# Three norms split around their turn: raw x is turned, weights enter at the turned block, the root at the product

## The reference

```python
def rms_norm(x, g):
    y = x * lax.rsqrt(jnp.mean(x * x, axis=-1, keepdims=True) + EPS)
    return y * g

# first block
h = rms_norm(x, norm_attn)
proj = h @ w_in                    # q_mla | ckv | k_rope | qkv_dil | gate_pre
o_mla, o_dil = mla_branch(...), dilated_branch(...)
gates = sigmoid(gate_pre + b_gate)
x = x + (gates[0] * (o_mla @ w_o_mla) + gates[1] * (o_dil @ w_o_dil)) @ w_out
h2 = rms_norm(x, norm_ffn)
x = x + hier_moe(h2, ...)          # router on h2: 4 groups, 32 experts, 2 per token

# second block, layer 0 even, layer 1 odd
h = h + attn_retention_mixer(rmsnorm(h, norm_mix[0]), even_w_in, even_w_out)
h = h + peer(rmsnorm(h, norm_ffn[0]), ...)     # 8 heads x 16 gathered rows per token
h = h + short_conv_mixer(rmsnorm(h, norm_mix[1]), ...)
h = h + peer(rmsnorm(h, norm_ffn[1]), ...)
return rmsnorm(h, final_norm)
```

## Time and profile before

| | |
|---|---|
| median of 3 runs | 2150.3 us (2147.6 to 2150.67) |
| profiled execution, its own time | 2149.94 us |
| span of the profiled execution | 2148.1 us |
| mean granted clock of TensorE | 0.970 |
| PE busy | 1849.5 us (86%) |
| DVE, ACT, POOL busy | 1285.7, 714.7, 663.4 us |
| chain that ended last | DMA 32%, DVE 17%, issue 9%, PE 8% |

### The profile page before, as it was taken

One profiled execution on the slowest core, in us unless ns is written; L12 is line 12 of the kernel. 1 busy time (PEld: TensorE's weight loads), 2 busy tenths in 40 slices (PEclk: granted clock), 3 DMA queues, 4 the chain that ended last, 5 costly groups with the idle time before them and its releaser, 6 DMA issues.

```text
span 2148.1 us, 20313 instructions
## 1 busy us (share of the span) xinstructions
PE 1849.5 (86%) x5992; PEld 871.0 (41%) x5992; DVE 1285.7 (60%) x3071; ACT 714.7 (33%) x2002; POOL 663.4 (31%) x593
## 2 busy tenths in 40 slices
PE   9999999997899999999868887677888867888876
PEld 4445555332245445454423333323433433334322
DVE  1333433221122768666478797987777888777765
ACT  1232221111111346344334333433333343444442
POOL 2121001110000334334334353454334345444432
PEclk9999999999999999999999999899999999999998
DMA  7432366999796999999999999999999999999996
GB/s 247 168 119 77 144 247 254 409 418 419 324 357 242 378 421 393 421 416 421 421 422 421 420 411 421 407 401 421 421 421 421 420 411 415 421 421 420 415 421 283
DMA packets 114801, 779.40 MB, mean 363 GB/s; under 512 B 16048, under 2 KB 17760, under 8 KB 21632
## 3 DMA queue, kind: packets, MB, share of 16 engines
q0 software_dynamic: 78928, 542.37, 61.4%
q1 hardware_dynamic: 32256, 225.65, 26.3%
q10 hardware_dynamic: 3504, 10.04, 1.2%
HBM read 780.10 MB, written 10.49 MB: 368 GB/s over the span
## 4 chain that ended last, share of the span: by engine, by line
DMA 32%; DVE 17%; issue 9%; PE 8%; POOL 5%; ACT 2%; DVEq 0%; POOLq 0%; ACTq 0%
DMA arena<-in_c_rows_dram,arena 32%; DVE arena L2732 8%; POOL arena L2829 5%; PE banks L2718 3%; PE banks L1824 2%; DVE x L2738 2%; PE banks L369 1%; DVE arena L2637 1%; DVE arena L2628 1%; PE banks L1915 1%; DVE arena L2631 1%; ACT arena L2795 1%; DVE arena L2673 1%; DVE arena L2666 1%; DVE arena L2670 1%
## 5 line engine op out<-in xcount | busy, mean ns | idle before, releaser
L2718 PE MATMUL banks<-arena 128*128 128x512 f32 x1784 | 892.2, 630 | 225.9 <-ACT arena L2795 222.4
L2829 POOL DMA_INDIRECT arena<-in_c_rows_dram,arena x512 | 585.8, 1144 | 839.9 <-PE banks L2718 481.8
L2732 DVE CUSTOM_DVE_ANT_0 arena<-arena,xn 128x1024 f32<-128x1024 f32 x512 | 625.8, 1223 | 302.0 <-DMA arena<-in_c_rows_dram,arena 296.8
L2718 PEld LDWEIGHTS banks<-arena 128*128 128x128 f32 x1784 | 320.6, 195 | 684.0 <-ACT arena L2795 414.9
L2786 ACT ACTIVATE small<-small 128x1 f32<-128x1 f32 x512 | 103.5, 202 | 732.7 <-DVE small L2732 728.7
L314 PE MATMUL banks<-ring,hT 128*128 128x512 f32 (+1 forms) x480 | 202.1, 577 | 0.0
L2795 ACT ACTIVATE arena<-ident,small 128x128 f32<-128x128 f32 x446 | 179.1, 401 | 42.0 <-ACT small L2789 1.5
L376 ACT COPY arena<-banks 128x512 f32<-128x512 f32 (+4 forms) x218 | 101.0, 492 | 254.9 <-PE banks L360 107.4
L2789 ACT ACTIVATE small<-small 128x1 f32<-128x1 f32 x512 | 150.8, 295 | 49.0 <-DVE arena L2644 0.4
L314 PEld LDWEIGHTS banks<-ring,hT 128*128 128x128 f32 x480 | 87.9, 191 | 100.2 <-issue 98.4
L402 POOL TENSOR_TENSOR small<-small 128x1 f32<-128x1 f32 (+4 forms) x24 | 33.4, 1391 | 285.1 <-DVE small L398 266.0
(11 more groups left out here) (319 smaller groups left out, 1799.9 us busy)
## 6 DMA issues: line engine op xcount, KB each, us to landing
arena<-in_c_experts_dram SPq DMA_DIRECT2D x51, 1024.0 KB, 20.1
ring<-in_c_w_in_dram SPq DMA_DIRECT2D x30, 1024.0 KB
ring<-in_c_experts_dram SPq DMA_DIRECT2D x30, 1024.0 KB
ring<-in_c_w_q_dram SPq DMA_DIRECT2D x18, 1024.0 KB
ring<-in_c_odd_w_in_dram SPq DMA_DIRECT2D x15, 1024.0 KB
ring<-in_c_even_w_in_dram SPq DMA_DIRECT2D x12, 1024.0 KB
arena<-in_c_even_w_in_dram SPq DMA_DIRECT2D x10, 1024.0 KB, 17.3
arena<-in_c_rows_dram,arena POOLq DMA_INDIRECT x512
```

The lines of the kernel that those rows point to most:

```text
L2718: r = e.matmul(banks[:, bank_of[("acc", L, c, hf)], :], diag[:, diag_of[m], :], rows[:, row_of[m], D + hf * 512:D + (hf + 1) * 512], start ...
L2732: e.tensor_tensor_reduce(u, u, xn[:, c, :], 1.0, 0.0, ALU.mult, ALU.add, hid3[:, c, h, k:k + 1]).then_inc(ve.sem, ve.up(("u", p)))
L2829: e.indirect_dma_start(rows[:, b, :], None, table_uv, bass.IndirectOffsetOnAxis(ap=eix[:, c, 16 * h + k:16 * h + k + 1], axis=0)).then_inc ...
```

## The change

Norms "attn", "ffn" and "mix0" are split. x itself is turned (`pe_turn_half`), the gain, now a value per partition of the turned block (`gT_all`, 12 KB, loaded once), is multiplied in when the turned block is copied to `hT` (`act_gained`, four operations of one block each; `dve_gained`, one operation of four blocks), and the root is multiplied in when the product's bank is emptied (`act_rooted`, `scalar_tensor_tensor` on VectorE). The row copies of the gain for "attn" and "mix0" are no longer loaded. For the stored rows of the router, VectorE writes x * gain by halves (`times_gain`) and ScalarE multiplies by the root (`normed`).

At the start the identity is loaded before x. In the router the first chunk's turn stands inside the third half product, its router product before the fourth, its choice beside the fourth, and the rank product between that product's two parts; four idle products behind the first router are gone. Before the even mixer three idle products behind the addition are gone.

```diff
+        def act_gained(e, n, c, k):
+            name = ("hT", n, c, k)
+            g = fetched("gains")
+            e.wait_ge(g.sem, g.at("all"))
+            e.wait_ge(pe.sem, pe.at(name))
+            for i in range(4):
+                e.activation(hT[:, k + i, c * P:(c + 1) * P], banks[:, bank_of[name], i * P:(i + 1) * P], ACT.Copy,
+                             scale=gain_T[n][:, k + i:k + i + 1]).then_inc(ac.sem, ac.up(name))
+
+        def dve_gained(e, n, c, k):
+            e.tensor_tensor(hT[:, k:k + 4, c * P:(c + 1) * P], turned(name, P, 4),
+                            gain_T[n][:, k:k + 4].unsqueeze(2).to_broadcast([P, 4, P]),
+                            ALU.mult).then_inc(ve.sem, ve.up(name))
+
+        def act_rooted(e, name, dst, src, n, c):
+            await_root(e, n, c)
+            e.wait_ge(pe.sem, pe.at(name))
+            e.activation(dst, src, ACT.Copy, scale=ssn[n][:, c:c + 1]).then_inc(ac.sem, ac.up(name))
...
             ready(e, 1)
-            a2 = half(1, 0)
+            a2 = half(1, 0, first_turned)
             rings.drop(a2)
-            pe_turn_chunk(e, n, 0, xn[:, 0, :])
-            mid0(e)
-            a3 = half(1, 512)
-            mid1(e)
+            router(e, 0)
+            a3 = half(1, 512, ranked)
             rings.drop(a3)
-            pe_turn_chunk(e, n, 1, xn[:, 1, :])
+            turn_added(e, 1, 0)
+            turn_added(e, 1, 4)
+            router(e, 1)
...
             add(0, 0)
+            times_gain(0, 0)
             add(0, 512)
-            dve_norm(e, n, 0)
+            times_gain(0, 512)
+            mean(0)
+            dve_gained(e, n, 0, 4)
             add(1, 0)
-            dve_turned_chunk(e, n, 0)
+            times_gain(1, 0)
+            chosen(e)
+            ranked(e)
             add(1, 512)
-            e.wait_ge(ac.sem, ac.at(("sq", n, 1)))
-            dve_mean(e, ssn[n][:, 1:2], D, ("ms", n, 1))
-            mid0(e)
-            dve_normed(e, n, 1)
-            mid1(e)
-            dve_turned_chunk(e, n, 1)
+            dve_gained(e, n, 1, 4)
+            mean(1)
+            times_gain(1, 512)
...
+            square(0)
+            act_gained(e, n, 0, 0)
+            normed(0)
+            act_gained(e, n, 1, 0)
+            chain(e, ac)
+            square(1)
+            normed(1)
...
             elif s == GAIN_AT:
-                e.wait_ge(ve.sem, ve.at(("xn", "ffn", 1)))
+                e.wait_ge(ve.sem, ve.at(("xg", "ffn", 1)))
+                e.wait_ge(ac.sem, ac.at(("sq", "ffn", 1)))
...
             pe_idle_work(e, "results", 8, still)
-            e.wait_ge(ve.sem, ve.at(("x", "mix0", 0)))
-            pe_idle_work(e, "results added", 3, still)
             tensor_even(e)
```

More of the change, by code:

```diff
@@ L442, in sp_residual, with pe_residual, half @@
                     load(e, ("res" + n, c0, k), w[c0 // 256 + k // 4])
-        def pe_residual(e, n, lhs, second, mid0, mid1, ready):
-            def half(c, c0):
+        def pe_residual(e, n, lhs, second, ready, router, ranked):
+            def half(c, c0, between=None):
                 name = ("res" + n, c0, "c", c)
@@ L483, in add, with times_gain, mean @@
                 emptied[name] = (ve.sem, ve.n)
+            def times_gain(c, c0):
+                g = fetched("gain_" + n)
+                e.wait_ge(g.sem, g.at("all"))
+                chain(e, ve)
+                e.tensor_tensor(xn[:, c, c0:c0 + 512], x[:, c, c0:c0 + 512], gain[:, gain_of[n], c0:c0 + 512],
+                                ALU.mult).then_inc(ve.sem, ve.up(("xg", n, c)))
+            def mean(c):
+                e.wait_ge(ac.sem, ac.at(("sq", n, c)))
+                dve_mean(e, ssn[n][:, c:c + 1], D, ("ms", n, c))
@@ L1006, in scalar_first @@
         def scalar_first(e):
-            gain_fetch(e, "attn")
+            g = fetched("gains")
+            e.dma_start(gT_all, a["c_gains"]).then_inc(g.sem, g.up("all", by=16))
             for c in range(2):
@@ L1414, in router @@
                 r.then_inc(pe.sem, pe.up(("lg", c)))
-            def first_router(e):
-                router(e, 0)
-                pe_idle_work(e, "norm", 4, still)
-            still = rw.rearrange("p k n -> p (k n)")
-            pe_residual(e, "ffn", hT, second, nothing, first_router, ready)
-            router(e, 1)
-            rings.drop(("lg", 0))
-            rings.drop(("lg", 1))
             def bank(name):
@@ L1428, in bank, with ranked @@
                 return b
-            b = bank(("rank", 0))
-            e.wait_ge(fetched("tri").sem, fetched("tri").at("all"))
-            e.wait_ge(po.sem, po.at("ones"))
-            e.wait_ge(ve.sem, ve.at(("Ms", 0)))
-            e.matmul(banks[:, b, 0:32], tri, Ms[:, 0, :], start=True, stop=True).then_inc(pe.sem, pe.up(("rank", 0)))
+            def ranked(e):
+                b = bank(("rank", 0))
+                e.wait_ge(fetched("tri").sem, fetched("tri").at("all"))
+                e.wait_ge(po.sem, po.at("ones"))
+                e.wait_ge(ve.sem, ve.at(("Ms", 0)))
+                e.matmul(banks[:, b, 0:32], tri, Ms[:, 0, :], start=True, stop=True).then_inc(pe.sem, pe.up(("rank", 0)))
+            still = rw.rearrange("p k n -> p (k n)")
+            pe_residual(e, "ffn", hT, second, ready, router, ranked)
+            rings.drop(("lg", 0))
+            rings.drop(("lg", 1))
             b = bank(("rank", 1))
@@ L1561, in whose_place, with chosen @@
                                          ALU.is_equal, ALU.mult), ("hots", c))
-            first = choose(0)
-            def some(n):
-                for _ in range(n):
-                    next(first, None)
-            dve_residual(e, "ffn", lambda e: some(3), lambda e: some(5))
-            for _ in first:
-                pass
-            e.wait_ge(po.sem, po.at("ids"))
-            whose_tile(0)
+            def chosen(e):
+                for _ in choose(0):
+                    pass
+                e.wait_ge(po.sem, po.at("ids"))
+                whose_tile(0)
+            dve_residual(e, "ffn", chosen, lambda e: whose_place(0))
             for _ in choose(1):
                 pass
-            whose_place(0)
             whose_tile(1)
```

134 lines of the change are left out of this document (87 added, 47 removed).

## The result

The changed kernel took 2151.97 us (median of 20 runs, 2148.57 to 2155.75), the kernel before 2147.97 in the same sessions (20 runs, 2145.44 to 2152.26). The ratio is 1.0015, with an interval (95%) of 1.0009 to 1.0022: slower by 0.15%, some 3.2 us (the two medians lie 4.0 apart). I had forecast 2.9 us faster. Single executions of either kernel spread over 7 us, so I read the places in the profiles, not only the end.

A forecast was written before the change was run, and what follows sets the result against it. TensorE was taken to bound the first block, weight DMA the experts, both the mixer; 0.9 - 0.3 + 1.8 + 0.5 = 2.9 us gained gave 2147.4 us, range 2142.3 to 2151.8.

The forecast's parts named there:

- Even mixer: Before the even mixer: TensorE gets 2.9 us ahead, then waits for columns 1024's load; 0.5 us gain kept.
- the loads of this stage start only when the results have landed, which the change does not move: Even mixer: weight loads start no earlier, so of TensorE's 2.9 us lead only 0 to 1.6 is left.
- Router: Router: earlier second choice and gather let TensorE turn rows 2.1 us earlier; 1.8 us gained, ends 4.5 gained and 1.6 lost.
- I take 5.8: Router: the first gather, sharing engines with 2 MB of loads, lands in 5.8 us, between 3.4 unloaded and 9.6 loaded.
- I take off 0.3: Router: allowance of 0.3 us for TensorE's lower clock, which could lengthen the first expert products by up to 1.7.
- the router gives nothing: Rival at the router: late store and gather among 2 MB take all the gain; 2149 to 2150.8 us, chance 0.20.
- The mixer's gain is kept: Rival at the even mixer: columns 1024 land well before TensorE, 2.9 us gained instead of 0.5; 2145.0 us, chance 0.26.
- Start: Attention norm at the start: turning raw x brings the first product from 11.22 to 10.3 us; 0.9 us gained.
- Scaled unloads: Bank unloads with the root: each ScalarE one costs 0.09 us more, mostly beside TensorE; 0.3 us lost.
- The waits that I had priced: Attention pairs: TensorE waits for ScalarE's copies 8 times for 3.7 us; scaled unloads there lose nothing to 1.5 us.
- that rival: Rival on ScalarE: scaled copies reload its table, 1.28 us per switch; 2159 us, chance 0.04.
- The fourth rival: Rival in the last 1440 us, a chain of row gathers: another load order costs some us; 2155 us, chance 0.06.

The follow-up runs named there:

- e5: Changed kernel with four loads not needed before 685 (2.0 MB) issued behind ScalarE's exponentials and unloads, not ahead of its first unload; ratio 1.0011.
- e8: Changed kernel with the even mixer's weight stream released when the first chunk's expert results have landed, not both chunks'; ratio 0.9991.
- e9: Kernel before with the even mixer's weight stream released by the first chunk's expert results alone; ratio 0.9994.
- e1: Kernel before with only the attention norm split, router and even mixer as before; ratio 0.9999.
- e3: Kernel before with only the even mixer's norm split and the three idle products left out; ratio 1.0009.
- e6: Kernel before with four loads (next norm's gain, keys, second mixer's gain, convolution's weights) moved behind ScalarE's exponentials and unloads; ratio 0.9999.
- e11: Changed kernel with the two 1 MB expert weight loads held until the first gathered rows have landed; ratio 0.9990.
- e2: Kernel before with only the router's norm split and its order changed; ratio 0.9997.
- e12: Changed kernel with both the two 1 MB loads held behind the first gather and the stream released by the first chunk's results; 2142.5 us, ratio 0.9964.

## Why the prediction was wrong

Four terms made the sum. The steps that failed are the mixer's release of the stream, and in the router the landing of the gather and the price of the clock.

- **Even mixer: 0.5 gained, in fact 2.3 lost in the profile (C to D), 2.0 on the mean (113.7 in nine kernels with it and the old release of the stream, 111.7 in six without).** The first half of the mechanism stood: TensorE came 3.0 us ahead and waited for columns 1024. What failed is "the loads of this stage start only when the results have landed, which the change does not move". Counted from C, which is what a head start of TensorE is counted from, it moved: the stream started 1.2 later. I also stopped at the first wait. The next tile that TensorE stood for, the second one of columns 2560, began 62.5 after C. Before, 60.4 after C was early enough (both tiles of 2560 run from 650.66 for 7.03 us without a wait). Some 0.6 of the rest may be ScalarE's loads, which go out earlier (e5); what remains is not explained. That the stream's release is the limit is shown by e8 against e9: 2.2 gained with it moved.
- **Router: 1.8 gained, in fact 1.3 lost at B, 1.7 on the mean (A to B 62.9 in eight kernels with it alone, from 60.3 to 63.7, and 61.2 in before, e1, e3, e6 and e9, from 59.7 to 61.9).** The chain up to the gather went as written: second store at 352.27, gather released by the store, issued 3.2 earlier after A on the mean (2.5 forecast). Two steps behind it failed. The first is the landing, "I take 5.8": from its issue to the turn it was 7.2 in the profile and 8.0 on the mean of the eight (up to 9.0). So the turn, 2.1 earlier by the forecast, came 1.65 earlier in the profile (50.8 after A and not 52.5) and 0.4 on the mean. The second is "I take off 0.3" for the clock. The idle products' weight loads ran at the full clock, took 4.18 us instead of the 6.93 that I had used, and left TensorE idle for 4.6. In the kernel before they had run at 0.50. Behind the wait it was the work that ran at 0.50: 0.94 lost on the turn, 1.06 on the products behind it, 0.98 on the up-projection, together 3.0 us (2.2 on the mean). The rival "the router gives nothing" was right in its outcome and, on the mean, in its reason (the late landing takes most of the gain); it did not foresee the clock. "The mixer's gain is kept" was not right. e11 shows that the two loads are what the gather waits for: held back, it is there in 3.5 us. The rule of the Trainium skill that loads of all issuers interleave on the same engines (DMA: Bandwidth & Descriptors, Issuing engines are not separate DMA queues) agrees with that 3.5 against 7.2.
- **Start: 0.9 gained, in fact 0.7 at the first product on the mean, of which 0.3 is left at A.** The two profiles alone show 0.05, because the end of the idle products, which I had read as fixed, lies between 7.3 and 8.8 from one execution to the next. The turn follows them directly, as forecast. The first product comes at 11.1 to 11.3 in the six kernels with the old start; with the new one it comes at 9.8 to 10.2 in the five whose granted clock from 20 to 40 us is 0.91, and at 10.6 to 11.2 in the six where it is 1.00. From there to A it took 303.9 with the old start and 304.3 with the new at 1.00, and 305.6 and 306.0 at 0.91, each within 0.03 in all kernels of its kind. So the lower clock costs 1.7 with either start, and it, not the change, makes the 1.36 by which A came earlier in the profile (0.05 at the first product, 0.4 lost on the way, 1.7 from the clock). At 0.91 A is at 316.7 with the old start (3 kernels) and 316.0 with the new (5), at 1.00 at 315.1 (3) and 315.2 (6).
- **Scaled unloads: 0.3 lost, in fact 0.4.** 683 ns against 587 on 128x512, the 0.09 forecast. The 0.4 is what the new start loses between the first product and A (above). All of it is lost between 131 and 300 us, among the attention pairs; that the unloads make it and not something else there is not shown. The waits that I had priced hardly grew (3.8 us in 8, before 3.7 in 8), but TensorE waited for ScalarE for another 0.8 and 0.5 us at two places where it had not before. Table loads are as many as before (35, 32, 3, 2 and single ones): that rival is out.

Together 1.7 + 2.0 - 0.3 (the start's 0.7 less the unloads' 0.4) = 3.4 us lost, against 3.2 measured. That it comes so close is partly luck: the router's term is uncertain by about 1, e2's total shows none of it, and A to C scatters by almost 5 with one router. The fourth rival, a drift of the last part, did not appear.

## What to carry over

- When a norm leaves TensorE's path, the next limit can be what starts the weight stream, as in the mixer here. Read which wait releases the first load of the stage, and move that release together with the norm: here one semaphore less turned 2.3 us lost into 2.2 gained between C and D.
- Work out a head start to the last tile that is waited for, not the first. If every stall is followed by another for the same queue, neither filling it nor saving the clock helps.
- A number of idle products fits one length of wait at one clock. An order that makes the wait start sooner needs the count set anew, and a load that is on the path belongs ahead of the big ones that merely may go out.

## What the runs showed of the hardware

- TensorE's clock from 20 to 40 us is granted at 0.91 in eight of the seventeen executions and at 1.00 in nine, with either start; the first makes the way to A 1.7 us longer, to within 0.03 us.
- Idle products at the lower clock can be the better cover of a wait. In e5 the 18 records took 7.17 us, the wait behind them was 1.87, and the expert products ran at the full clock (7.09); in the changed kernel they took 4.61, the wait was 4.58, and they ran partly at the lower (8.07). Which of the two a run gets was not steered by any edit (low in e5 and e12 among the kernels with the new router, full in e6 among those with the old one). Where the wait is short, low ones are the worse cover: A to B is 58.2 in e12 and 56.1 in e11.
- ScalarE's queue held up its own work by 1.8 to 2.3 us for each load issued while the engines were full (four issues from 615.46 on in the changed kernel, first unload at 624.38), and by 1.5 to 2.7 us in the kernel before. Taking it away gave 0.6 us from C to D at most (e5) and 0.1 in the kernel before (e6).
- A load of 1 MB can be late by its last few per cent: the second result load was not complete until 606, though the engines' share was only 0.07 and 0.02 in the two us before. What held it is not shown.
